# Twelve of 128 first keys of a product-key expert layer computed densely instead of gathered

## What is computed

```python
q = (xt @ w_q).reshape(T, H, 2, 128)                  # T = 256 tokens, H = 8 heads
s = jnp.einsum('thcd,hcnd->thcn', q, sub_keys)        # 128 first keys, 128 second keys
top_s, top_i = lax.top_k(s, 16)
cand   = top_s[:, :, 0, :, None] + top_s[:, :, 1, None, :]
cand_i = top_i[:, :, 0, :, None] * 128 + top_i[:, :, 1, None, :]
best_s, best_j = lax.top_k(cand.reshape(T, H, 256), 16)
expert = take(cand_i, best_j)                         # 16 of 16384 small experts a head
g = softmax(best_s)
act = gelu(einsum('cd,chkd->chk', xc, u_tab[expert])) # one dot of 1024 with each expert's u row
out = einsum('chk,chkd->cd', g * act, v_tab[expert])  # weighted sum of the v rows
```

## Time and profile before

| | |
|---|---|
| profiled execution, own time | 1509.36 us |
| its span, first to last instruction | 1507.6 us |
| TensorE matmuls busy | 1248.3 us (83%) |
| VectorE busy | 761.6 us (51%) |
| ScalarE busy | 476.1 us (32%) |
| GpSimd busy | 278.8 us (18%) |
| DMA | 544.11 MB, mean 361 GB/s |
| last layer's gathers | from 839 us to the end |

### The profile page before, as it was taken

The page is one execution under the profiler, slowest core; times in us unless marked ns, Lnnn a source line. Parts: engine busy times, 40 slices in busy tenths (PEclk is TensorE's granted clock), DMA queues, the critical chain, the costliest instruction groups (busy, mean ns, idle before and its releaser), DMA issues.

```text
span 1507.6 us, 21173 instructions
## 1 busy us (share of the span) xinstructions
PE 1248.3 (83%) x8468; PEld 736.4 (49%) x8468; DVE 761.6 (51%) x1804; ACT 476.1 (32%) x1246; POOL 278.8 (18%) x294
## 2 busy tenths in 40 slices
PE   7999999999999998999999977787665655565655
PEld 7787555656565556977766644354311111111112
DVE  5744222212112115567852885677566665767444
ACT  5933010111010015356742344333323232323223
POOL 0000000000000001101000333344434343433331
PEclk9999999999999999999999998999968677767679
DMA  9548999999999999543451799999999999999997
GB/s 392 205 178 346 428 424 426 424 425 424 424 426 424 426 425 373 214 169 139 165 241 56 280 424 420 420 407 420 421 421 421 420 422 420 421 421 420 422 421 280
DMA packets 65016, 544.11 MB, mean 361 GB/s; under 512 B 6672, under 2 KB 7184, under 8 KB 13200
## 3 DMA queue, kind: packets, MB, share of 16 engines
q1 hardware_dynamic: 26592, 273.85, 44.3%
q0 software_dynamic: 38016, 268.45, 43.1%
q10 hardware_dynamic: 304, 0.39, 0.1%
HBM read 541.62 MB, written 1.05 MB: 360 GB/s over the span
## 4 chain that ended last, share of the span: by engine, by line
PE 46%; DMA 36%; DVE 6%; issue 5%; ACT 4%; POOL 2%; POOLq 0%; DVEq 0%; SPq 0%; ACTq 0%
PE PS L205 45%; DMA AR<-in_uv,CO 27%; DMA AR<-in_w_up 7%; PE PS L215 2%; DVE AR L2455 2%; DMA EX<-in_w_up 1%; DMA Wk<-in_w_up 1%; POOL AR L2706 1%; DVE LO L201 1%; ACT Wk L2350 0%; ACT HI L194 0%; ACT SM L2344 0%; POOL AR L2678 0%; DVE Wk L1778 0%; DMA CO<-in_const 0%
## 5 line engine op out<-in xcount | busy, mean ns | idle before, releaser
L205 PE MATMUL PS<-AR,Wk 64*64 64x512 f32 (+3 forms) x2040 | 374.8, 742 | 168.8 <-ACT Wk L2350 149.4
L2455 DVE CUSTOM_DVE_ANT_0 AR<-AR,PS 128x1024 f32<-128x1024 f32 x193 | 234.9, 1220 | 163.7 <-DMA AR<-in_uv,CO 157.9
L205 PEld LDWEIGHTS PS<-AR,Wk 64*64 64x64 f32 (+3 forms) x2040 | 100.7, 160 | 396.0 <-ACT Wk L2350 252.7
L2706 POOL DMA_INDIRECT AR<-in_uv,CO x186 | 180.0, 968 | 280.6 <-PE PS L205 245.8
L205 PE MATMUL PS<-AR 128*64 128x256 f32 (+3 forms) x1656 | 194.5, 385 | 7.1 <-DMA AR<-in_w_up 3.4
L205 PEld LDWEIGHTS PS<-AR 128*64 128x64 f32 (+3 forms) x1656 | 122.0, 139 | 85.6 <-issue 22.3
L316 POOL TENSOR_TENSOR ST<-ST 128x2 f32<-128x2 f32 (+3 forms) x14 | 12.8, 915 | 774.2 <-DVE ST L1178 480.6
L2340 ACT ACTIVATE RW<-SM 128x2 f32<-128x2 f32 (+1 forms) x132 | 26.9, 204 | 407.3 <-DVE SM L2455 371.6
L201 DVE TENSOR_TENSOR LO<-AR,HI 128x1024 fp32r<-128x1024 f32 x84 | 100.6, 1238 | 37.6 <-ACT HI L194 37.5
L1054 DVE TENSOR_TENSOR AR<-AR,PS 128x256 f32<-128x256 f32 x32 | 13.5, 421 | 192.5 <-ACT AR L905 192.5
L205 PE MATMUL PS<-Wk,AR 128*128 128x128 f32 (+2 forms) x816 | 95.9, 310 | 2.0 <-ACT Wk L1966 1.1
(11 more groups left out here) (342 smaller groups left out, 1855.4 us busy)
## 6 DMA issues: line engine op xcount, KB each, us to landing
AR<-in_w_up SPq DMA_DIRECT2D x24, 2048.0 KB, 14.7
AR<-in_w_down SPq DMA_DIRECT2D x24, 2048.0 KB, 14.7
AR<-in_w_gate SPq DMA_DIRECT2D x24, 2048.0 KB, 14.7
AR<-in_w_in SPq DMA_DIRECT2D x13, 2048.0 KB, 9.8
EX<-in_w_gate SPq DMA_DIRECT2D x4, 2048.0 KB, 14.7
Wk<-in_w_up SPq DMA_DIRECT2D x4, 2048.0 KB, 14.7
EX<-in_w_down SPq DMA_DIRECT2D x4, 2048.0 KB, 14.7
Wk<-in_w_gate SPq DMA_DIRECT2D x4, 2048.0 KB, 14.9
```

Of the source, the lines that this page charges most:

```text
L205: return pe.matmul(o, l, r, start=start, stop=stop, skip_group_check=True)
L2455: t = dve.tensor_tensor_reduce(r, r, P(6 if g < 128 else 2, 2), 1.0, 0.0, ALU.mult, ALU.add, DT[:, g:g + 1])
L2706: pool.indirect_dma_start(RING[k], None, uv, bass.IndirectOffsetOnAxis(ap=IDX[:, g:g + 1], axis=0)).then_inc(g_in[k], 16)
```

## The change

Experts whose first key is 116 to 127 (12 of 128) are no longer gathered. Their tables are loaded whole, and each of these 12 x 128 experts is computed for all tokens:

- `u0` to `u11`: a load of 128 u rows (0.5 MB, from a copy `ut` of these rows laid out in 8 x 128 pieces), 8 matmuls against the tokens of both blocks (`XD`, 256 columns), a gelu by ScalarE into `HD`. Batches 45 to 63.
- `turn`, `id`, `first`, `hot`, `w`, `at`: for each token, a 128 x 12 matrix of shares is built from the chosen experts. VectorE makes one-hot tiles of the second and the first key (the latter multiplied by the share), TensorE multiplies them token by token (8 tokens a step, 16 steps a block), and VectorE multiplies `HD` by the result. Batches 65 to 84 for block 0, 95 to 108 for block 1.
- `v0` to `v11`: a load of 128 v rows (0.5 MB), 8 matmuls that add to the sums of both blocks. Batches 109 to 123.

The shares are split after each softmax: `BG` keeps those of gathered experts, `BS` those of dense ones, the other being zero (`shares_apart`). The gathers get a bound, beyond which a row is left out; a slot then keeps old contents in that row, with share zero. The dots write their products to a buffer outside the ring, so each waits for the one before. Slots 9 and 0 no longer join the ring (12 slots at the end); `CHOSEN_FROM` has the later choices earlier. The squares of block 0 come at batch 125 and its output after all dots, as its sums are complete only then.

```diff
+DENSE = 12
+FETCHED = 128 - DENSE
-        JUNKE = AR[:, at7 + 3072:at7 + 4096]
+        PRODUCTS = (CS4[1].rearrange("p h n -> p (h n)"), JUNK[1])
+        DENSE_ROWS = [EX8[:, 1024 * k:1024 * k + 1024] for k in range(4)]
...
         GROWS = {0: (2, ...), 3: (1, ...), 5: (7, ...), 46: (4, ...), 62: (5, ...),
-                 72: (3, k_pe.at("q11b")), 82: (9, k_pe.at("q21b")), 92: (0, k_pe.at("q31b"))}
+                 72: (3, k_pe.at("q11b"))}
...
+        U_AT = [45 + 16 * i * 12 // (10 * DENSE) for i in range(DENSE)]
+        HOT_FROM, V_AT = (68, 98), [109 + 13 * i * 12 // (10 * DENSE) for i in range(DENSE)]
+        def hot_at(tt, n):
+            return HOT_FROM[tt] + (n // 2 if tt else n)
...
+        def dense_load(sp, name, of):
+            n = STREAM.index(name)
+            sp.wait_ge(*(d_pe.at(STREAM[n - 4]) if n >= 4 else k_pe.at("q21b")))
+            sp.dma_start(DENSE_ROWS[n % 4], of).then_inc(dense_in[n % 4], 16)
...
+                o = P(1 - i % 2)[:, 0:256].rearrange("p (t n) -> p t n", t=2)      # u
+                matvec(pe, o, lambda c: u[:, c, :], lambda c: XD[:, c], 8).then_inc(*d_pe.up(name))
...
+                pe.wait_ge(*d_dve.at(f"hot{tt}.{n}"))                              # w
+                for k in range(8):
+                    at = (n % 4 * 8 + k) * DENSE
+                    t = mm(pe, P(7 - q % 2)[:, at:at + DENSE], SECOND_HOT[n % 2][:, k, :], FIRST_HOT[:, 8 * n + k, :], True, True)
...
+                for tt in range(2):                                                # v
+                    for r in range(2):
+                        at = 128 * tt + 64 * r
+                        for j in range(2):
+                            t = mm(pe, sums_at(tt, r)[64 * j:64 * j + 64, :], HD[:, i, at:at + 64], v[:, 512 * j:512 * j + 512], False, False)
...
+                if n >= 2:                                                         # hot
+                    dve.wait_ge(*d_pe.at(f"w{tt}.{n - 2}"))
+                shape = [128, 8, 128]
+                dve.tensor_tensor(SECOND_HOT[n % 2], bc(SECOND[:, 8 * n:8 * n + 8].unsqueeze(2), shape), bc(co["iota"].unsqueeze(1), shape),
+                                  ALU.is_equal).then_inc(*d_dve.up(name))
...
                 dve.wait_ge(g_in[place_of[g]], 16 * uses[g])
-                t = dve.tensor_tensor_reduce(r, r, P(6 if g < 128 else 2, 2), 1.0, 0.0, ALU.mult, ALU.add, DT[:, g:g + 1])
-            t.then_inc(*batches.up())
+                if g:
+                    dve.wait_ge(*products.at())
+                dve.tensor_tensor_reduce(PRODUCTS[10 <= b < 16], r, P(6 if g < 128 else 2, 2), 1.0, 0.0, ALU.mult, ALU.add,
+                                         DT[:, g:g + 1]).then_inc(*products.up())
...
+        def shares_apart(dve, fetched, dense, first, nh):
+            first = first.rearrange("p (h k) -> p h k", h=nh)
+            dve.scalar_tensor_tensor(dense, first, float(FETCHED), fetched, ALU.is_ge, ALU.mult).then_inc(*own.up())
+            dve.wait_ge(*own.at())
+            return dve.scalar_tensor_tensor(fetched, first, float(FETCHED), fetched, ALU.is_lt, ALU.mult)
...
-        CHOSEN_FROM = [0, 5, 16, 28, 44, 60, 76, 92]
+        CHOSEN_FROM = [0, 5, 16, 28, 40, 54, 68, 82]
-        TOTAL_AT, MEAN_AT, SCALED_AT, POWER_AT = 65, 76, 106, 190
+        TOTAL_AT, MEAN_AT = 125, 129
...
-                    pool.indirect_dma_start(RING[k], None, uv, bass.IndirectOffsetOnAxis(ap=IDX[:, g:g + 1], axis=0)).then_inc(g_in[k], 16)
+                    pool.indirect_dma_start(RING[k], None, uv, bass.IndirectOffsetOnAxis(ap=IDX[:, g:g + 1], axis=0),
+                                            bounds_check=128 * FETCHED - 1, oob_is_err=False).then_inc(g_in[k], 16)
```

More of the change, by code:

```diff
@@ L73, in program @@
 def program(nc, x, const, small, rows, w_in, w_sp, w_out, w_r, w_gate, w_up, w_down, mem, w_in2, ck1, ck2,
-            w_a, w_b, w_out2, w_cq, w_ckv, w_co, w_pq, subk, uv, gp, fin2, out):
+            w_a, w_b, w_out2, w_cq, w_ckv, w_co, w_pq, subk, uv, ut, gp, fin2, out):
     with ExitStack() as ctx:
@@ L2224, in program, with by_batch @@
         uv2 = uv.rearrange("e (t d) -> (e t) d", t=2)
+        U_AT = [45 + 16 * i * 12 // (10 * DENSE) for i in range(DENSE)]
+        HOT_FROM, V_AT = (68, 98), [109 + 13 * i * 12 // (10 * DENSE) for i in range(DENSE)]
+        def hot_at(tt, n):
+            return HOT_FROM[tt] + (n // 2 if tt else n)
+        def by_batch(pairs):
+            at = {}
+            for b, name in pairs:
+                at.setdefault(b, []).append(name)
+            return dict(sorted(at.items()))
+        DENSE_PE = by_batch([(42, "wide"), *((b, f"u{i}") for i, b in enumerate(U_AT)), (65, "turn0"), (95, "turn1"),
+                             *((hot_at(t, n), f"w{t}.{n}") for t in range(2) for n in range(16)), *((b, f"v{i}") for i, b in enumerate(V_AT))])
@@ new lines, in program @@
+        DENSE_ACT = by_batch((min(b + 2, 63), f"u{i}") for i, b in enumerate(U_AT))
+        DENSE_DVE = by_batch([(44, "xd"), (65, "id0"), (67, "first0"), (95, "id1"), (97, "first1"),
+                              *((hot_at(t, n), f"hot{t}.{n}") for t in range(2) for n in range(16)),
+                              *((hot_at(t, 4 * q + 3) + 3, f"at{t}.{q}") for t in range(2) for q in range(4))])
+        d_pe, d_act, d_dve = (Steps(sem(n), [x for names in at.values() for x in names])
+                              for n, at in (("d_pe", DENSE_PE), ("d_act", DENSE_ACT), ("d_dve", DENSE_DVE)))
@@ new lines, in dense_act, with dense_dve @@
+        def dense_act(act, name):
+            i = int(name[1:])
+            act.wait_ge(*d_pe.at(name))
+            act.activation(HD[:, i, :], P(1 - i % 2)[:, 0:256], ACT.Gelu).then_inc(*d_act.up(name))
+        def dense_dve(dve, name):
+            if name == "xd":
+                dve.wait_ge(*d_pe.at("wide"))
+                for tt in range(2):
+                    t = dve.tensor_tensor(XT[tt], XT[tt], bc(P(0)[:, 128 * tt:128 * tt + 128].unsqueeze(1), [128, 8, 128]), ALU.mult)
+                t.then_inc(*d_dve.up("xd"))
+            elif name[:2] == "id":
+                tt = int(name[2])
+                if tt:
+                    dve.wait_ge(*d_pe.at("w0.15"))
+                else:
+                    dve.wait_ge(*k_pe.at("key31"))
+                    dve.wait_ge(p_pool.sem, 4)
+                dve.tensor_copy(PLACES, IDX[:, 128 * tt:128 * tt + 128]).then_inc(*d_dve.up(name))
+            elif name[:2] == "fi":
+                tt = int(name[5])
+                dve.wait_ge(*d_pe.at(f"turn{tt}"))
+                dve.tensor_copy(SHARE, P(6)[:, 128:256])
+                dve.tensor_scalar(FIRST, P(6)[:, 0:128], 1.0 / 128, -63.5 / 128, ALU.mult, ALU.add).then_inc(*own.up())
+                dve.wait_ge(*own.at())
+                dve.tensor_scalar(FIRST, FIRST, WHOLE, None, ALU.add).then_inc(*own.up())
+                dve.wait_ge(*own.at())
+                dve.tensor_scalar(FIRST, FIRST, WHOLE, None, ALU.subtract).then_inc(*own.up())
+                dve.wait_ge(*own.at())
+                dve.scalar_tensor_tensor(SECOND, FIRST, -128.0, P(6)[:, 0:128], ALU.mult, ALU.add)
+                shape = [128, 128, DENSE]
+                dve.tensor_tensor(FIRST_HOT, bc(FIRST.unsqueeze(2), shape), bc(co["iota"][:, FETCHED:128].unsqueeze(1), shape),
+                                  ALU.is_equal).then_inc(*own.up())
+                dve.wait_ge(*own.at())
+                dve.tensor_tensor(FIRST_HOT, FIRST_HOT, bc(SHARE.unsqueeze(2), shape), ALU.mult).then_inc(*d_dve.up(name))
+            elif name[0] == "h":
+                tt, n = int(name[3]), int(name[5:])
+                if n >= 2:
+                    dve.wait_ge(*d_pe.at(f"w{tt}.{n - 2}"))
+                elif n == 0 and not tt:
+                    dve.wait_ge(*d_dve.at("first0"))
+                shape = [128, 8, 128]
+                dve.tensor_tensor(SECOND_HOT[n % 2], bc(SECOND[:, 8 * n:8 * n + 8].unsqueeze(2), shape), bc(co["iota"].unsqueeze(1), shape),
+                                  ALU.is_equal).then_inc(*d_dve.up(name))
+            else:
+                tt, q = int(name[2]), int(name[4])
+                at = 128 * tt + 32 * q
+                dve.wait_ge(*d_pe.at(f"w{tt}.{4 * q + 3}"))
+                if tt == 0 and q == 0:
+                    dve.wait_ge(*d_act.at(f"u{DENSE - 1}"))
+                h = HD[:, :, at:at + 32].rearrange("p i t -> p t i")
+                w = P(7 - q % 2)[:, 0:32 * DENSE].rearrange("p (t i) -> p t i", i=DENSE)
+                dve.tensor_tensor(h, h, w, ALU.mult).then_inc(*d_dve.up(name))
@@ L2235, in peer_sp @@
             load_piece(sp, "pq3")
-            sp.wait_ge(*k_pe.at("q30b"))
+            for i in range(DENSE):
+                dense_load(sp, f"u{i}", ut[i])
+            sp.wait_ge(*d_pe.at(f"u{DENSE - 1}"))
             for j in range(2):
                 sp.dma_start(FIN[64 * j:64 * j + 64, :], fin2[64 * j:64 * j + 64, 512 * j:512 * j + 512]).then_inc(ld_fin, 16)
```

(14 more changed lines are left out.)

84 lines of the change are left out of this document (76 added, 8 removed).

## The result

The changed kernel takes 1541.86 us (median of 4 runs, 1539.15 to 1543.64), against 1509.53 for the kernel before: 1.0206 times its time, 95% interval 1.0192 to 1.022. Forecast was 1503, range 1488 to 1522. The profiled execution took 1539.15 us.

What follows compares the result with a forecast made beforehand. DMA engines, each at its own limit on the last layer's row gathers, were taken as the bound. From 1509.4 us: -40 rows left out, +30 loads, +1 second block, +2 start, +1 end gives 1503.4; forecast 1503, range 1488 to 1522.

Steps and rivals of the forecast that it cites:

- The bound: Last layer's row gathers: all 16 DMA engines busy from about 860 to 1490 us at 420 GB/s, each at its own limit.
- Rows left out, -40: Gathers: 2894 rows (23.7 MB) not fetched; the fullest engine sets the pace, 2.33 us per gather, saving 40 us.
- Loads, +30: 12 loads of u and 12 of v, 12.58 MB while DMA is already full, cost 29.9 us.
- TensorE, w: Batches 68 to 83 hidden beside DMA; in 98 to 105, TensorE 51 us beside DMA's 37, 14 us late, counted +1.
- rival B: Batches 98 to 105: TensorE sets the pace through dearer weight loads, perhaps at the low clock; +16, 1519; chance 0.17.
- The ring's reserve, 18: Ring of 12 slots, 28 us around: consumers may be 18 us late before the DMA queue runs empty.
- TensorE, u and v: Batches 45 to 62 (u, 83 us beside DMA's 99) and 109 to 123 (v, 73 beside 80): both hidden.
- VectorE: One-hot tiles 1.22 us each; 6 us late in batches 68 to 83, made good later; hidden in 98 to 105.
- GpSimd: Gather issue takes 0.95 us; with a bound to check, up to 2.3 us changes nothing; nothing added.
- Start 2, end 1: First gathers: split and waits, 2 us (1 to 4); end: first block's late scaling and stores, 1 us (0 to 3).
- A: Gathers: rows shared evenly, or engines' drift hides the fullest one; -56 in place of -40, 1487 to 1490; chance 0.17.
- C: Gathers: a row out of bounds still takes its engine's time, so nothing is saved; 1543 us; chance 0.06.

Runs made afterwards that it cites:

- e9: Changed kernel without dense part and without the gathers' bound, so every row is gathered; ring of 12, waits and split shares kept: 1512.34 us.
- e4: Changed kernel without its dense part (no loads, u, w, v); gathers with the bound, ring of 12, waits and split shares kept: 1477.16 us.
- e7: e4 plus the 24 loads of the dense tables (12.58 MB), with nothing that uses them: 1508.43 us.
- e1: Changed kernel with 128 moving columns instead of 12 in the w steps' matmuls of both blocks: 1515.16 us.
- e5: Changed kernel with 128-column w steps, the second block's steps one to a batch, and 3 filler matmuls instead of 8: 1512.85 us.
- e11: Changed kernel with the sums of the batch's second gather put between its two w steps in the second block, still 12 columns: 1555.23 us.
- e3: Changed kernel with seven of eight matmuls of each of the second block's w steps left out, one-hot tiles kept: 1512.73 us.
- e10: e9 with all rows left out in every 11th gather (2944 rows, the same number for every DMA engine): 1463.88 us.
- e2: Changed kernel with the second block's w steps one to a batch (96 to 111) and v in batches 113 to 124: 1515.87 us.
- e8: e4 with slots 9 and 0 back in the ring, 16 slots as in the kernel before: 1478.57 us.

## Why the prediction was wrong

The runs add up to the changed kernel's time: 1510.3 before, +2.0 ring, waits and split (e9), -35.2 rows left out (e4), +31.3 loads (e7), +6.7 the dense work at the high clock (e1), +26.7 the same with 12 columns, where the clock falls: 1541.8. Each term is the difference of two neighbouring runs, so the sum has to come out; what counts are their sizes. Of the 38 us between the forecast and the measured time 27 are the w steps at the low clock. The other 12 are terms sized too small: rows 5, loads 1, the dense work at the high clock 5 (6.7 for the 1 + 1 of the sum), and 1 in the starting point. By the steps:

- **The bound**: right. DMA set the time before, and does so in e5.
- **Rows left out, -40**: right in kind (the fullest engine, a pace of 2.33 us and 411 GB/s), a little large: -35.2. The even case, 184 rows an engine or 57 us by the same count, also gave less, 48.5. The part before batch 36 is not all DMA's: at 1000 to 1020 us e4 has a share of 0.87 with TensorE busy 18.07 of 20, where the ring grows from 8 to 10 slots and the queries of later heads run. That this is the whole of the missing 5 us is not shown.
- **Loads, +30**: right, 31.3.
- **TensorE, w**: this step failed. I priced a record at 0.14 us from rows of early layers, where the clock was high, and counted 51 us for batches 98 to 105. Measured are 75.3: three batches with w steps of 4.0 to 4.2 us, five with 7.00 and sums of 3.69. The term of the sum is +1 at the second block; it measured 26.7 (changed kernel less e1), and some 3 more that e1 still lost there. What I put wrong was the argument against rival B, that the change makes TensorE busier and so its clock higher. Busy it was, 20.00 of 20, and at 0.50.
- **The ring's reserve, 18**: too large. The eight batches were 38 us late and DMA lost 30, so the ring held 8. e1 gives 7 (10 late, 3 lost) and e11 some 11 (52 late, 41 lost). With 18, DMA would have lost 20. Why the reserve is so much smaller than I worked out was not taken apart.
- **TensorE, u and v**: right. DMA stays full beside u (1.01 to 1.02 at 1100 to 1200 us), and beside v (1.01 at 1440 to 1520), at a clock of 1.00.
- **VectorE**: the hot tile was 1223 ns for 1.22. In the second block it was not on the path (e3).
- **GpSimd**: an issue with a bound took 1.03 us for 0.95, unimportant; the changed kernel's page has 1033 ns.
- **Start 2, end 1**: e9 has 2.0 for start, waits and split together.
- **Rivals**: A was wrong, by e4 against e10. C was wrong, by the 35 us of e4 against e9, though its number, 1543, is what came out: two mechanisms gave the same time, and only the bytes and stages tell them apart. B was right in place and in kind. With everything at the low level I had 76 us for the eight batches, and they took 75.3; that is in part luck, as three of them ran at the high level and the rest were dearer than I had it (3.69 for 3.43, 0.22 a record for 0.19). I had not taken that price but a middle one (+16), gave B 0.17, and subtracted 18 us of reserve in place of 8.

## What to carry to other kernels

Price a new matmul at both clock levels, and ask whether it streams columns: a stage of weight loads with 12 columns each left the clock low here though the engine never idled, and padding the moving side up to what a weight load takes was faster, not slower. Where a stage can run at either level, one profiled execution isn't enough: look at the spread of all, as in e2. Measure how late consumers can be before the DMA queue runs dry, instead of taking it from the number of slots. Where a transfer leaves rows out, count them for each DMA engine, not in all. And work out what the best case is worth before the work is placed: here 35 us of rows against 31 us of loads left nothing to win.

## What the runs showed of the hardware

- 32 f32 records with 12 columns took 7.00 us at a granted clock of 0.50 and 4.00 to 4.22 at 1.00, with 128 columns 3.84 at 1.00. With 12 columns both levels occurred, the low one for up to 99 us (e11) with the engine busy nearly all the time; with 128, in e1's second block, it was 1.00 for all the w steps (1364 to 1408 us).
The Trainium skill, TensorE: Matmul & The Clock Gate, Part 1: The HAM clock gate, says that a monitor sets the clock by how busy the array has been. If this is read as the busy time of matmuls in the profile, the trace does not agree: 20.00 of 20 us busy at 0.50.
- An indirect transfer that leaves rows out keeps its number of packets (38016) and drops their bytes, and nearly all their time (9 ns for 0.31 us a row).
- One engine's spare time is no use to another: 420 GB/s with even rows (e10), 411 with uneven ones (e4; the fullest engine 2.5% above the mean if each takes 8 neighbouring tokens). With more slots the rate was 418 and the time the same (e8).
